# A transformer block on one core: each stage's first loads issued in the stage before it

## The chip, the cores and the metric

The kernel runs on one core of one Trainium2 chip. The metric is the device time in microseconds of one execution; the median of three runs counts. The engines are PE (TensorE, matrix products; PEld its weight loads), DVE (VectorE), ACT (ScalarE), POOL (GpSimd) and SP (SyncE, which here only issues DMAs, in the order of its program). They meet through semaphores.

## What is computed

One block on x of 1024 tokens by 1024 features, in float32: a half-weighted FFN, a mixer made of sparse attention (8 heads of 64) and an RWKV-7 recurrence (8 heads of 64), cross attention to 256 memory tokens, and a second FFN. Cut to what matters:

```python
x = x + 0.5 * rms_norm(swiglu(rms_norm(x, g), w_gate, w_up, w_down), g_post)      # FFN 1, D_FF 2816
proj = rms_norm(x, mix_pre_g) @ w_in                                              # 25 chunks of 128 columns
o_nsa  = nsa_mixer(q, k_c, v_c, k_s, v_s, k_w, v_w, gate_logits, ...)             # keys and queries rotated
o_rwkv = rwkv7_mixer(r, k, v, w_lo, a_lo, g_lo, ...)                              # (y + bonus) * g
x = x + rms_norm(concat([rms_norm(o_nsa, nsa_out_g), o_rwkv]) @ w_out, mix_post_g)
m = rms_norm(mem, mem_kv_g)
x = x + rms_norm(memory_cross_attention(rms_norm(x, mem_pre_g), m, wq, wk, wv, wo), mem_post_g)
x = x + 0.5 * rms_norm(swiglu(rms_norm(x, g), w_gate, w_up, w_down), g_post)      # FFN 2
```

## The kernel before

Every dense product is made of three passes of PE: each operand is split into a high part (ACT casts it) and a low part (DVE subtracts the high part from the original), and high x high, high x low and low x high are summed. So no product starts before its weights are loaded, cast by ACT and subtracted by DVE.

The work is in five stages, each a block of one program per engine, each with its own tiles in SBUF and its own semaphores: FFN 1 (`ffn_products`, L103), the front (`project_and_prepare`, L1756), attention with the recurrence (`attend_and_recur`, L1042), the memory stage (`memory_tail`, L2543) and FFN 2. Between two stages `Core.clear` (L66) sets the stage's semaphores back to zero on four engines, in a block of its own; a stage ends only when SP has waited for all of its stores. `block_kernel` (L2938) calls them.

FFN: SP loads a pair of 2 x 1 MB (256 columns of w_gate and of w_up, `load_pair`, L248) into `raw`, then loops over 11 pairs. FFN 2 begins with it. In FFN 1 the last loop (L319 to L326) goes over eight tiles of x: store tile t, load tile t + 3; DVE adds, normalises, and PE transposes for the next stage.

Front: 41 chunks of weights, 0.5 MB each, loaded by `load` (L1869) into two `raw` buffers in turn; a load waits until DVE has done the subtraction of the chunk two before. Chunks 0 to 24 are w_in, for all 1024 tokens (48 matmuls of 512 columns each). Chunks 25 to 32 are mem_wv and 33 to 40 mem_wk, for the 256 memory tokens (24 matmuls of 256 columns each). Rotated keys and queries, the recurrence's operands (`ops`, four of them), its values, gates and bonus are stored to DRAM for the stages behind. The transposed and split memory tokens lie in the first 256 columns of `hi` and `lo`. The memory keys are stored by one DMA when all chunks are done (L1961: waits for 41 evictions), the memory values (vm) by one of 1 MB after two transposes. After its first subtraction DVE waits for 14 small vectors (`first_steps`, L2286). The order on every engine is that of a plan (`front_plan`), which a list scheduler makes out of events with durations and dependences; SP's order too. `tail_plan` does the same for the memory stage, `joint_plan` for attention.

Attention: SP loads the recurrence's operands of two chunks of 64 tokens (eight DMAs of 128 KB), the first queries (four), keys (four of 0.5 MB) and compressed keys `kc` (two), values `vs` and `vw`, `vc`, V of two chunks (four DMAs), the second and third queries (eight). ACT issues seven small mask loads and four larger ones. PE's order begins with the products `gram_b` of chunks 0 and 1, `gram_k`, `gram_l`, three turns, then `x`, which needs V, and then the first scores, which need queries and keys. DVE waits for all seven masks before its first operation.

Memory stage: product 0 to 3 multiply the mixed tokens with w_out (8 slabs of 0.5 MB, two `raw` buffers), each of them with 8 slabs x 4 banks x 3 matmuls; 4 to 7 are the queries, 8 to 11 the output. Before product 0, DVE and ACT mix the tokens in four quarters (`mix_o`, `mix_y`, `mix_hi`, `mix_lo`), with gate and bonus loaded by quarter. All products use the same four PSUM banks, so product n waits for the evictions of n - 1 (L2678). `load_x` of tile 0 (L2640) brings two gain rows, km, vm and x, 3.5 MB in all.

## Time and profile before

| | us |
|---|---|
| three runs: lowest, median, highest | 2912.26, 2913.5, 2915.74 |
| the profiled execution | 2917.97 |
| its span, first to last instruction | 2916.2 |
| PE busy in it | 2721.9 |
| DVE, ACT busy | 1752.2, 969.1 |

Times of the profile are microseconds from the start of the span; a line of a timeline gives its start, its length, the engine, the source line, the operation, and in brackets how long the engine had been idle before it and what released it. SPq and ACTq are DMA issues. The granted clock of PE is its mean over a stretch, 1.00 being 2.4 GHz and 0.50 1.2 GHz. The mean over the execution is 0.959.

### The profile page before, as it was taken

How to read it: one execution, taken by the hardware profiler on the slowest of the kernel's cores; microseconds unless marked ns; L12 is line 12 of the kernel's file. 1: busy time of each engine (PE TensorE's matmuls, PEld its weight loads, DVE VectorE, ACT ScalarE, POOL GpSimd, SP SyncE). 2: the span in 40 equal slices, each digit the busy share in tenths (PEclk: the TensorE clock that was granted, in tenths of full speed). 3: DMA queues.
4: the chain of work that ended last, by engine and by line, in shares of the span. 5: the costliest groups of instructions: out<-in, count | busy, mean ns of one | idle time of the engine just before them, and what ended most of it. 6: DMA issues, size and time to landing. Idle time of an engine off the chain costs nothing. (4 is left out here: it accounts for less than half of the span.)

```text
span 2916.2 us, 47485 instructions
## 1 busy us (share of the span) xinstructions
PE 2721.9 (93%) x19432; PEld 2237.5 (77%) x19432; DVE 1752.2 (60%) x2865; ACT 969.1 (33%) x1732; POOL 87.2 (3%) x120
## 2 busy tenths in 40 slices
PE   6999999998899999589999998599996999999998
PEld 5888887886677778578888887477775788887887
DVE  5866666677243373267777775653453866666766
ACT  4322222214323343234444443342342322222112
POOL 0000000000000000111111110000000000000000
PEclk9999999999799999889999999799997999999999
DMA  3222223223422374621111100640112122223324
GB/s 135 80 86 87 83 79 108 87 101 145 94 73 79 109 242 128 169 71 42 35 35 35 35 9 5 213 150 2 44 71 91 61 80 83 86 83 109 112 89 151
DMA packets 230380, 260.65 MB, mean 89 GB/s; under 512 B 63300, under 2 KB 186435, under 8 KB 230212
## 3 DMA queue, kind: packets, MB, share of 16 engines
q1 hardware_dynamic: 228628, 256.65, 27.4%
q8 instruction: 124, 2.03, 0.3%
q10 hardware_dynamic: 1584, 1.60, 0.2%
q14 instruction: 44, 0.36, 0.0%
HBM read 188.91 MB, written 64.06 MB: 87 GB/s over the span
## 5 line engine op out<-in xcount | busy, mean ns | idle before, releaser
L709 PE MATMUL f_ps<-f_t1h,f_wh 128*128 128x512 f32 x480 | 187.1, 390 | 0.0
L710 PE MATMUL f_ps<-f_t1l,f_wh 128*128 128x512 f32 x480 | 186.7, 389 | 0.0
L2013 PE MATMUL fr_dense_ps<-one_hi,fr_wh 128*128 128x512 f32 x400 | 170.9, 427 | 11.3 <-DVE fr_wl L2298 11.3
L709 PE MATMUL f_ps<-two_hi,f_wh 128*128 128x512 f32 x384 | 150.6, 392 | 19.0 <-DVE f_wl L495 15.7
L2015 PE MATMUL fr_dense_ps<-one_hi,fr_wl 128*128 128x512 f32 x400 | 159.6, 399 | 0.0
L2014 PE MATMUL fr_dense_ps<-one_lo,fr_wh 128*128 128x512 f32 x400 | 159.6, 399 | 0.0
L709 PE MATMUL f_ps<-one_hi,f_wh 128*128 128x512 f32 x384 | 151.1, 394 | 8.7 <-DVE f_wl L495 4.6
L709 PE MATMUL f_ps<-f_t2h,f_t3h 128*128 128x512 f32 x384 | 151.1, 393 | 7.7 <-DVE ffn_y L601 3.7
L711 PE MATMUL f_ps<-one_hi,f_wl 128*128 128x512 f32 x384 | 150.7, 392 | 0.0
L710 PE MATMUL f_ps<-one_lo,f_wh 128*128 128x512 f32 x384 | 150.6, 392 | 0.0
L711 PE MATMUL f_ps<-f_t2h,f_t3l 128*128 128x512 f32 x384 | 150.4, 392 | 0.0
L710 PE MATMUL f_ps<-f_t2l,f_t3h 128*128 128x512 f32 x384 | 150.3, 392 | 0.0
L710 PE MATMUL f_ps<-two_lo,f_wh 128*128 128x512 f32 x384 | 150.1, 391 | 0.0
L711 PE MATMUL f_ps<-two_hi,f_wl 128*128 128x512 f32 x384 | 149.9, 390 | 0.0
L2687 PE MATMUL mt_d_ps<-mt_wh,two_hi 128*128 128x512 f32 x256 | 108.2, 423 | 33.9 <-DVE two_lo L2877 23.5
L603 DVE TENSOR_TENSOR y<-f_ps,y 128x512 f32<-128x512 f32 x144 | 99.2, 689 | 62.1 <-PE f_ps L711 62.1
L343 ACT CAST f_wh<-f_raw 128x1024 fp32r<-128x1024 f32 x60 | 63.0, 1053 | 219.5 <-PE f_ps L711 208.3
L543 DVE TENSOR_TENSOR y<-f_ps,y 128x1024 f32<-128x1024 f32 x60 | 72.5, 1222 | 100.6 <-PE f_ps L711 100.6
L543 DVE TENSOR_TENSOR ffn_y<-f_ps,ffn_y 128x1024 f32<-128x1024 f32 x60 | 72.5, 1222 | 100.4 <-PE f_ps L711 100.4
L603 DVE TENSOR_TENSOR ffn_y<-f_ps,ffn_y 128x512 f32<-128x512 f32 x144 | 98.7, 689 | 56.0 <-PE f_ps L711 56.0
L711 PE MATMUL f_ps<-f_t1h,f_wh 128*128 128x512 f32 x320 | 124.5, 389 | 0.0
L2298 DVE TENSOR_TENSOR fr_wl<-fr_raw,fr_wh 128x1024 fp32r<-128x1024 f32 x41 | 50.1, 1222 | 99.0 <-ACT fr_wh L2169 99.0
(391 smaller groups left out, 6820.8 us busy)
## 6 DMA issues: line engine op xcount, KB each, us to landing
f_raw<-in_ffn_w_gate SPq DMA_DIRECT2D x22, 1024.0 KB, 5.4
f_raw<-in_ffn_w_up SPq DMA_DIRECT2D x22, 1024.0 KB, 7.8
f_raw<-in_ffn_w_down SPq DMA_DIRECT2D x22, 1024.0 KB, 4.8
f_raw<-act SPq DMA_DIRECT2D x22, 1024.0 KB, 4.8
fr_raw<-in_w_in SPq DMA_DIRECT2D x25, 512.0 KB, 4.0
act<-ffn_y SPq DMA_DIRECT2D x44, 256.0 KB, 2.0
act<-y SPq DMA_DIRECT2D x44, 256.0 KB, 2.0
arena<-x SPq DMA_DIRECT2D x16, 512.0 KB, 4.0
```

Of the source, the lines that this page charges most:

```text
L343: nc.scalar.copy(w_hi[:, SLOT[s]], operand(s)).then_inc(split_hi, 1)
L543: nc.vector.tensor_tensor(out, a, b, op).then_inc(joined, 1)
L603: nc.vector.tensor_tensor(y[part(m)], down_bank(m), y[part(m)], ALU.add).then_inc(added[m % 4], 1)
L709: nc.tensor.matmul(out, wh, xh, start=start, stop=False)
L710: nc.tensor.matmul(out, wh, xl, start=False, stop=False)
L711: return nc.tensor.matmul(out, wl, xh, start=False, stop=stop)
L2013: nc.tensor.matmul(dense_ps[:, b, cols], w_hi[:, b, k, :], hi[:, k, cols], start=(k == 0), stop=False)
L2014: nc.tensor.matmul(dense_ps[:, b, cols], w_hi[:, b, k, :], lo[:, k, cols], start=False, stop=False)
L2015: mm = nc.tensor.matmul(dense_ps[:, b, cols], w_lo[:, b, k, :], hi[:, k, cols], start=False, stop=(k == KD - 1))
L2298: nc.vector.tensor_tensor(w_lo[:, c % 2], raw[:, c % 2], w_hi[:, c % 2].bitcast(F32), ALU.subtract).then_inc(lo_split, 1)
L2687: mm = nc.tensor.matmul(dense_ps[b][:], lhsT[:, k, at], rhs[:, k, to], start=(k == 0 and x_ == 0), stop=(k == KD - 1 and x_ == 2))
```

## The change

Each stage gets a function `lead` that its SP program calls near its end, and that issues the first loads of the next stage. They signal on semaphores made by `lasting`, which no `clear` resets, and write to tiles that outlive the stage. In particular:

- FFN 1, after the store of x tile 1: the first two weight chunks of the front, into `y[:, 0:2]`, which is now the front's `raw` (its `krv` lies in the rest of `y`).
- Front, behind the loads of chunks 33 to 39: operands of chunk 0, operands of chunk 1 (four DMAs each), keys high, keys low (two DMAs of 0.5 MB each), queries 0, 1, 2 (four DMAs each). SP waits once, behind load 33, for 25 products and for the stores of operands and rotated rows. Keys and queries go into `hi`, so the memory tokens now lie in columns 0 to 511 of `lo`.
- Memory keys are stored chunk by chunk (eight DMAs of 128 KB), each after its own eviction.
- Attention, after its last loads: gate and bonus of quarter 0, slabs 0 and 1 of w_out and the two gain vectors of the memory stage.
- Memory stage, after the first store of its second round: the first pair of FFN 2.
- Memory stage: four slab buffers (two of them the former operand tiles), the companions of `load_x` tile 0 planned behind slab 7, and product 1 in the banks `pair_ps`, `t_ps`, `o_ps`; product 2 then waits for the evictions of product 0, and the first transpose for those of product 1.

```diff
-    def pool_dma_sems(self, name, n):
+    def lasting(self, name, n=1):
         return [self.nc.alloc_semaphore(name=f"{name}{i}") for i in range(n)]
...
-            load_pair(0)
+            if not begun:
+                load_pair(0)
...
                 sp.dma_start(x_out[of_tile(t), :], x_of(t)).then_inc(x_stored[t % 4], 16)
+                if t == 1 and lead is not None:
+                    lead(sp)
...
-                sp.dma_start(raw[:, c % 2], weights[:, :, COLS[c]:COLS[c] + P]).then_inc(raw_in[c % 2], 16)
+                if c >= 2:
+                    sp.dma_start(raw[:, c % 2], weights[:, :, COLS[c]:COLS[c] + P]).then_inc(raw_in[c % 2], 16)
+                if c == CHUNKS - 8:
+                    sp.wait_ge(multiplied, PROJECTED)
+                    for n in range(3):
+                        sp.wait_ge(op_stored[n], 16 * PAIRS)
+                    for b in range(2):
+                        sp.wait_ge(r_stored[b], 32)
+                        sp.wait_ge(rot_stored[b], 96)
+                if c >= CHUNKS - 8:
+                    lead(sp, c - (CHUNKS - 8))
...
-                    sp.wait_ge(evacuated, CHUNKS)
-                    sp.dma_start(km.rearrange("(c p) t -> p c t", p=P), km_sb).then_inc(mem_stored, 16)
+                    p = e[1]
+                    sp.wait_ge(evacuated, at[("memk", p)] + 1)
+                    sp.dma_start(km[p * P:(p + 1) * P, :], km_sb[:, p, :]).then_inc(mem_stored, 16)
...
-        event(("load_w", m), "sp", 0.5, m >= 2 and ("w_lo", m - 2), m and ("load_w", m - 1), late=3.0)
+        event(("load_w", m), "sp", 0.5 if m >= 2 else 0.0, m >= 4 and ("w_lo", m - 4), m and ("load_w", m - 1), late=4.0 if m >= 2 else 0.0)
...
-                event(("dense", n, k, b), "pe", 0.68, before, *ready, k == 0 and n and ("evac", n - 1, b))
+                room = k == 0 and n and n != 1 and ("evac", 0 if n == 2 else n - 1, b)
+                event(("dense", n, k, b), "pe", 0.68, before, *ready, room)
...
-                  idx == 0 and ("mix_y", QUARTERS - 1), r and ("stored", 0, t), late=3.0)
+                  idx == 0 and ("mix_y", QUARTERS - 1), idx == 0 and ("load_w", KD - 1), r and ("stored", 0, t), late=3.0)
...
+        raw = [raw01[:, 0, :], raw01[:, 1, :], ops[:, 0, :], ops[:, 1, :]]
...
+        def bank(n, b):
+            return (pair_ps[:, 0, :], pair_ps[:, 1, :], t_ps[:], o_ps[:])[b] if n == 1 else dense_ps[b][:]
...
+                    if n == TT:
+                        sp.wait_ge(scored, 32)
+                        sp.wait_ge(lo_split, 3 * KD)
+                        lead(sp)
...
+            def first_chunks(sp, y):
+                w_in = f["w_in"].rearrange("(k p) n -> p k n", p=P)
+                for c in range(2):
+                    sp.dma_start(y[:, c, :].rearrange("p (k n) -> p k n", n=P), w_in[:, :, COLS[c]:COLS[c] + P]).then_inc(chunk_in[c], 16)
+            def first_keys(sp, n):
+                if n < 2:
+                    AR, B, K = (x[n] for x in chunk_ops(ops))
+                    for which, dst in enumerate((AR[:, :, 0, :], B, K, AR[:, :, 1, :])):
+                        load_op(sp, n, which, dst, ops_dram, ops_in)
+                elif n < 4:
+                    load_keys(sp, n - 2, (rot_hi, rot_lo)[n - 2], hi, keys_in)
+                elif n < 7:
+                    load_queries(sp, n - 4, hi, rot_hi, rot_lo, q_in)
+            def first_mix(sp):
+                kv0, raw01 = early_parts(early)
+                for n, src in enumerate((gate_y, bonus_y)):
+                    sp.dma_start(kv0[:, n, :].rearrange("p (q t) -> p q t", q=PAIRS),
+                                 src.rearrange("(q p) t -> p q t", p=P)[:, :, 0:QW]).then_inc(mix_in[0], 16)
+                for m in range(2):
+                    sp.dma_start(raw01[:, m, :], f["w_out"][m * P:(m + 1) * P, :]).then_inc(slab_in[m], 16)
...
+            def first_pair(sp):
+                for n, w in enumerate((f["ffn2_w_gate"], f["ffn2_w_up"])):
+                    sp.dma_start(early[:, n], w.rearrange("(k p) n -> p k n", p=P)[:, :, 0:2 * P]).then_inc(pair_in, 16)
```

## Rows read from the trace of the kernel before

**Rows 1.** The page: busy time by engine, and a DMA issue (count, KB, landing).

```profile
PE 2721.9 (93%) x19432; PEld 2237.5 (77%) x19432; DVE 1752.2 (60%) x2865; ACT 969.1 (33%) x1732; POOL 87.2 (3%) x120
...
act<-ffn_y SPq DMA_DIRECT2D x44, 256.0 KB, 2.0
```

**Rows 2.** Who PE waited for: us in total, times, longest.

```profile
PE f_ps L709 <- DVE f_wl L495: 20.3, 2, 15.7
PE ar_ps L1327 <- DMA ar_AR<-ops: 19.2, 2, 14.6
```

**Rows 3.** Timeline, FFN 1 to front, the first load, cast, product, and DVE's wait.

```profile
738.39 0.39 SPq L1873 DMA_DIRECT2D fr_raw<-in_w_in  x1
742.67 1.04 ACT L2169 CAST fr_wh<-fr_raw 128x1024 fp32r<-128x1024 f32 x1 [7.88 <-DMA fr_raw<-in_w_in]
745.03 0.79 PE L2013 MATMUL fr_dense_ps<-one_hi,fr_wh 128*128 128x512 f32 x1 [11.35 <-DVE fr_wl L2298]
750.16 0.17 DVE L2288 TENSOR_SCALAR fr_mu<-fr_mu 128x14 f32<-128x14 f32 x1 [5.18 <-DMA fr_vecs<-in_rwkv_gn_b]
```

**Rows 4.** Timeline, last two evictions of the front, store, attention's first issues.

```profile
1202.05 0.37 ACT L2179 COPY fr_c_w<-fr_dense_ps 128x256 f32<-128x256 f32 x1 [1.12 <-PE fr_dense_ps L2036]
1205.42 0.37 ACT L2179 COPY fr_c_w<-fr_dense_ps 128x256 f32<-128x256 f32 x1 [2.99 <-PE fr_dense_ps L2036]
1205.82 0.37 SPq L1962 DMA_DIRECT2D km<-fr_c_w  x1
1213.74 0.42 ACTq L1493 DMA_DIRECT2D ar_m_gram<-in_m_gram  x1
1216.72 0.45 ACTq L1493 DMA_DIRECT2D ar_mean_all<-in_mean_all  x1
```

**Rows 5.** Timeline of attention's ramp: DVE's first two evictions, product x.

```profile
1222.10 0.69 DVE L1554 TENSOR_TENSOR ar_GB<-ar_ps,ar_m_gram 128x512 f32<-128x512 f32 x1 [19.91 <-PE ar_ps L1327]
1228.60 0.69 DVE L1554 TENSOR_TENSOR ar_GB<-ar_ps,ar_m_gram 128x512 f32<-128x512 f32 x1 [5.81 <-PE ar_ps L1327]
1244.20 1.97 PE L1327 MATMUL ar_ps<-ar_V,ar_GK 64*64 64x64 f32 x32 [9.61 <-DMA ar_V<-rv_tok]
```

**Rows 6.** DMA issues (KB, landing), 1160 to 1206; then windows (busy, clock, share, GB/s).

```profile
fr_raw<-in_mem_wk SPq DMA_DIRECT2D x8, 512.0 KB, 4.0
...
vm<-fr_krv SPq DMA_DIRECT2D x1, 1024.0 KB, 5.3
km<-fr_c_w SPq DMA_DIRECT2D x1, 1024.0 KB, 4.7
...
1180.00:1190.00 10.00, 5.38 (x38) 4.97 (x37) 2.45 (x2) 2.24 (x5) 0.00 (x0) 0.93 0.80 215
```

**Rows 7.** Timeline, attention to memory stage, and around the gap in product 0.

```profile
1821.92 1.06 ACT L2782 ACTIVATE arena<-arena 128x1024 f32<-128x1024 f32 x1
1826.82 3.26 DVE L2860 SCALAR_TENSOR_TENSOR y<-y,mt_gain,arena 128x256 f32<-128x256 f32 x8 [7.86 <-DMA mt_g_pre<-in_mem_pre_g]
1841.08 0.76 PE L2687 MATMUL mt_d_ps<-mt_wh,two_hi 128*128 128x512 f32 x1 [23.51 <-DVE two_lo L2877]
...
1856.17 0.69 SPq L2639 DMA_DIRECT2D mt_raw<-in_w_out  x1
1868.72 1.23 DVE L2887 TENSOR_TENSOR mt_wl<-mt_raw,mt_wh 128x1024 fp32r<-128x1024 f32 x1 [9.22 <-ACT mt_wh L2803]
1870.00 0.79 PE L2687 MATMUL mt_d_ps<-mt_wh,two_hi 128*128 128x512 f32 x1 [9.02 <-DVE mt_wl L2887]
```

**Rows 8.** Timeline and windows, memory stage to FFN 2: first load, cast, PE's rate.

```profile
2221.12 0.38 SPq L250 DMA_DIRECT2D f_raw<-in_ffn_w_gate  x1
2229.47 3.88 ACT L334 CAST f_wh<-f_raw 128x1024 fp32r<-128x1024 f32 x4 [11.08 <-DMA f_raw<-in_ffn_w_up]
...
2233.00:2237.00 4.00, 4.00 (x10) 3.18 (x11) 2.17 (x2) 1.63 (x2) 0.00 (x0) 0.56 0.15 29
2237.00:2245.00 8.00, 8.00 (x37) 6.61 (x36) 0.00 (x0) 0.00 (x0) 0.00 (x0) 1.00 0.76 250
```

More of the change, by code:

```diff
@@ L121, in ffn_products @@
     with core.stage() as ctx:
-        raw = sbuf(nc, ctx, f"{tag}_raw", [P, 2, KD, 2 * P])
+        begun = raw is not None
+        if not begun:
+            raw, raw_in = sbuf(nc, ctx, f"{tag}_raw", [P, 2, KD, 2 * P]), core.sem(f"{tag}_raw_in")
         w_hi = sbuf(nc, ctx, f"{tag}_wh", [P, 4, 2, 4, P], F32R)
@@ L274, in _ @@
                     load_first(t)
-            load_pair(0)
+            if not begun:
+                load_pair(0)
             if before:
@@ L1039, in joint_plan, with queries_of, chunk_ops, load_op @@
     return in_order(engine, takes, needs, tiling=tiling)
+def queries_of(hi):
+    return hi[:, 4:7, :].rearrange("p r (w h t) -> p r w h t", w=2, h=4)
+def chunk_ops(ops):
+    parts = [ops[:, j, :].rearrange("p (x c) -> p x c", c=CH) for j in range(2)]
+    return ([x[:, 0:2 * PAIRS].rearrange("p (q w) c -> p q w c", w=2) for x in parts], [x[:, 2 * PAIRS:3 * PAIRS] for x in parts],
+            [x[:, 3 * PAIRS:4 * PAIRS] for x in parts])
+def load_op(sp, c, which, dst, ops_dram, ops_in):
+    src = ops_dram[which].rearrange("(q p) t -> p q t", p=P)[:, :, c * CH:(c + 1) * CH]
+    sp.dma_start(dst, src).then_inc(ops_in[c % 2], 16)
+def load_queries(sp, g, hi, rot_hi, rot_lo, q_in):
+    for w, rot in enumerate((rot_hi, rot_lo)):
+        src = rot[g % 2 * 4 * DH:(g % 2 + 1) * 4 * DH, g // 2 * P:(g // 2 + 1) * P].rearrange("(h d) t -> d h t", d=DH)
+        for half in range(2):
+            sp.dma_start(queries_of(hi)[half * CH:(half + 1) * CH, g % 3, w].bitcast(F32), src).then_inc(q_in[g % 3], 16)
+def load_keys(sp, w, rot, hi, keys_in):
+    for n, row in enumerate((4 * P, 5 * P)):
+        src = rot[row:row + 2 * DH, :].rearrange("(g d) t -> d g t", d=DH)
+        sp.dma_start(hi[w * CH:(w + 1) * CH, 2 * n:2 * n + 2, :].bitcast(F32), src).then_inc(keys_in, 16)
 def attend_and_recur(core, tag, rot_hi, rot_lo, kc_hi_dram, kc_lo_dram, v_tok, vc_dram, gates,
-                     ops_dram, rv_dram, end_decay, consts, a, hi, oT, o_ms, yT, y_var):
+                     ops_dram, rv_dram, end_decay, consts, a, hi, oT, o_ms, yT, y_var,
+                     ops, ops_in, keys_in, q_in, lead):
     nc = core.nc
@@ L1169, in _ @@
         def _(sp):
-            def load_q(g):
-                for w, rot in enumerate((rot_hi, rot_lo)):
-                    src = rot[g % 2 * 4 * DH:(g % 2 + 1) * 4 * DH, of_tile(g // 2)].rearrange("(h d) t -> d h t", d=DH)
-                    for half in range(2):
-                        sp.dma_start(q[rows(half), g % 3, w].bitcast(F32), src).then_inc(q_in[g % 3], 16)
-            def load_op(c, which, dst):
-                src = ops_dram[which].rearrange("(q p) t -> p q t", p=P)[:, :, chunk(c)]
-                sp.dma_start(dst, src).then_inc(ops_in[c % 2], 16)
             def load_v(c):
@@ L2540, in tail_plan, with early_parts, memory_tail @@
     return in_order(engine, takes, needs, lag)
-def memory_tail(core, tag, a, oT, o_ms, yT, y_var, arena, gate_dram, bonus_dram, x1, x2, x3, km, vm, hi, lo, y, consts):
+def early_parts(early):
+    return [early[:, n].rearrange("p (a k) f -> p a (k f)", a=2) for n in range(2)]
+def memory_tail(core, tag, a, oT, o_ms, yT, y_var, arena, gate_dram, bonus_dram, x1, x2, x3, km, vm, hi, lo, y, consts,
+                early, ops, vectors, mix_in, raw_in, gain_in, g_pre_in, lead):
     nc = core.nc
@@ L2572, in memory_tail @@
         top, bias, den, rden = (small[:, n, :] for n in range(4))
-        gate = kv[:, 0:2, :].rearrange("p r (q t) -> p r q t", q=PAIRS)
-        bonus = kv[:, 2:4, :].rearrange("p r (q t) -> p r q t", q=PAIRS)
-        kT = kv[:, 0:2, :].rearrange("p a (c t) -> p (a c) t", t=MT)
-        v = kv[:, 2:4, :]
+        kv0, raw01 = early_parts(early)
+        raw = [raw01[:, 0, :], raw01[:, 1, :], ops[:, 0, :], ops[:, 1, :]]
+        gate, bonus = ([kv[:, n, :].rearrange("p (q t) -> p q t", q=PAIRS) for kv in (kv0, kv1[:])] for n in range(2))
+        kT = kv0.rearrange("p a (c t) -> p (a c) t", t=MT)
+        v = kv1[:]
+        gain, g_pre = vectors[:, 0:PAIRS], vectors[:, PAIRS:PAIRS + KD]
         x = arena[:, 0:2, :]
@@ L2959, in block_kernel @@
     core = Core(nc)
-    def hidden_pair(ctx, name):
-        return [sbuf(nc, ctx, f"{name}_{part}", [P, KD, T], F32R) for part in ("hi", "lo")]
     with ExitStack() as ctx:
@@ L2974, in block_kernel @@
             end_decay = sbuf(nc, mixer, "end_decay", [P, PAIRS, NCH])
+            vectors = sbuf(nc, mixer, "vectors", [P, PAIRS + KD])
+            ops = sbuf(nc, mixer, "chunk_ops", [P, 2, D])
+            hi = sbuf(nc, mixer, "hi", [P, KD, T], F32R)
+            chunk_in, ops_in, q_in, mix_in = (core.lasting(*n) for n in (("chunk_in", 2), ("ops_in", 2), ("q_in", 3), ("mix_in", 2)))
+            slab_in, (keys_in, gain_in, g_pre_in, pair_in) = core.lasting("slab_in", 4), core.lasting("early_in", 4)
```

148 lines of the change are left out of this document (71 added, 77 removed).

## The prediction

> **What bounds the kernel now.** I read the page first, then who waited for whom on PE, then the timeline at the four places where one stage hands over to the next, and last the DMA view of two of these. The page shows PE busy for 2721.9 of 2916.2 us [rows 1]: inside the stages it is full, and nothing in the diff takes matmuls away. What can move is the idle PE time, at most 194 us. The waits of PE name few causes [rows 2], and the timeline puts the long ones at the hand-overs: 11.35 us between FFN 1 and the front stage (A) [rows 3], 14.59 + 4.63 + 9.61 us between the front stage and attention (B) [rows 4, 5], 23.51 us and then 9.02 us at the start of the memory stage (C) [rows 7], 15.7 us before FFN 2 (D) [rows 2]. A hand-over is: last evacuation, the wait for stores, the clearing of semaphores, the first loads, the first splits. The change takes the loads out of this sequence. So I price each place by the engine that starts first once the loads are there.
>
> **A, FFN 1 to front.** The first two weight chunks are loaded in FFN 1's tail. Now SP issues the first at 738.39 and ACT's cast begins at 742.67, released by that DMA [rows 3]. ACT leaves the hand-over when SP does, so the cast moves forward by 742.67 - 738.39 = 4.3 us, the DVE subtraction and PE with it. Next to be late is DVE: after its first subtraction it waits for the 14 small vectors, until 750.16 [rows 3], and only then splits chunk 1. Those are still queued on SP behind where the two loads stood, so they are issued 1 to 3 us earlier, chunk 1 is ready at 751 at the latest, and PE has 48 matmuls of chunk 0 to do, over 11 us from 740.8 (the rate of [rows 8]). Covered. In FFN 1 the two loads (1.0 us of SP's queue, 1 MB) stand between a store of x and the load of x tile 4, which is added three tiles later, some 15 us; covered too, bound 2 us. Gain 4.3, between 2 and 4.6.
>
> **B, front to attention.** Three pieces.
> First the end: km, 1 MB, is stored at once after the last evacuation, issued 1205.82 and landed 4.7 later [rows 4, 6], so at 1210.5; the next stage starts 3.2 later, 1213.74 [rows 4]. By chunks the last store is 128 KB. The nearest row, 256 KB stores, land in 2.0 [rows 1]. I take 2.1: start at 1211.1, 2.6 earlier. Only that last one stands before a wait. The Trainium skill (DMA: Bandwidth & Descriptors, Bandwidth) asks for DMAs batched to 1 MiB or more, since small ones are dominated by fixed costs, which speaks against eight small stores; for the one that is waited for the rows disagree, 2.0 against 4.7.
> Second the ramp. With operands, keys and three groups of queries in place, PE's first products start at once. But DVE waits for the seven mask loads, which stay in this stage: the last is issued 2.98 after the start (1216.72) [rows 4] and DVE's first product is at 8.36 after it, at the latest then [rows 5]. I take 7.0 (5 to 8.4): 1218.1. From there the chain to the product x is as now: 0.7 for one more eviction, and from DVE's second at 1228.60 to PE's x at 1244.20 without its 9.61 wait for V, 6.0 [rows 5]. x at 1224.8 in place of 1244.20: 19.4 us. V must be in by then: its four loads stand behind two kc, two value and one vc load, no longer behind 20 others; issued about 6 after the start at 0.6 each, landing some 4 to 7 later, just in time. Their lateness is in the range.
> Third the price. 24 extra DMAs, 4.5 MB (operands 1, keys 2, queries 1.5) go on SP's queue between the weight loads of the last eight memory chunks, each group behind load c and ahead of load c+1. There two evictions are 3.4 us apart [rows 4], and a 0.5 MB load takes 4.0 to land, two buffers deep [rows 6], so there is hardly any slack: landing + cast 1.04 + subtraction 1.23 [rows 3, 7] is 6.3 for the 6.7 of two chunks. The row that shows what a bulk transfer ahead of a weight load does is that of vm: one store of 1 MB, 5.3 us, and in the 10 us behind it PE is busy for 5.38 at 215 GB/s [rows 6]. So a group of 1 MB costs up to 4.6 us of PE, and there are two such (keys), and five of 0.5 MB. Counted as bytes from the first of these loads: weights 4.2 MB, vm 1, km chunks 0.9, groups 4.5, 10.6 MB, at 215 GB/s [rows 6] 49 us, at 250 [rows 8] 42 us, where eight chunks of 3.4 and vm's hole of 4.6 make 32 us now; but what is queued behind the last weight load doesn't delay it, and not every group finds the queue full. Followed step by step, each transfer behind the one before (0.5 MB 2.0 us; 1 MB 3.4, vm's landing less the 2.0 that a landing holds beyond its transfer), I get the last weights 6 us later. I take 7 us of delay, 2 to 15. The Trainium skill, same page, Queues, rings and completion order, says each DMA engine consumes descriptors in ring order: with it a weight load does wait behind the group; the vm row agrees. SP's new wait at chunk 33 (25 products done, operands and rotated rows stored) is over long before by the same plan; behind it stand that group and load 34. Net 19.4 - 7 = 12.4 us, between 4 and 19.
>
> **C, attention to memory stage.** Gate, bonus, the gains and two slabs of w_out are already in. DVE starts now at 1826.82, released by the gain load; ACT's square root, the other input, begins 1821.92 and takes 1.06 [rows 7]. So DVE can start at 1823.1: 3.7 us. Then the 9.02 us stall: slab 6 is issued at 1856.17 behind two row gains, km, vm and x, 3 MB, and its product starts at 1870.00 [rows 7]. After the change x and its companions come behind slab 7, and four buffers let slabs run four ahead, so that wait goes; what is late next is DVE, which stood idle for 9.22 us there and is full before it [rows 7]. DVE's end of the eight slabs thus moves by 3.7 + 9.2 = 12.9. After a stall PE also runs its first 4 us at half clock: granted 0.56, 10 matmuls, where 8 us at 1.00 hold 37 [rows 8], so a stall costs 4 - 10 x 8/37 = 1.8 us on top. Some of that comes back: I take 13.5. The other banks for product 1 let it start without the evictions of product 0; no wait of before stands there, so nothing, and the added wait, first transposes behind product 1's evictions, has some 40 us of matmuls to hide in. Ends: 9 (the planner puts transposes and slabs less well), 20 (it brings product 0 ahead of the second quarter's mixing, three DVE passes of 1.23 and half of one of 3.26 [rows 7]).
>
> **D, memory stage to FFN 2.** The pair of 1 MB each is issued at 2221.12, ACT's cast starts 2229.47, released by it [rows 8]. With the pair in place the cast starts with the stage: 8.3 us, 7 to 9. The loads go out near the first store of round two, where nothing but x tiles, due over 20 us later, is queued behind.
>
> **Sum.** 4.3 + 12.4 + 13.5 + 8.3 = 38.5 us. The profiled execution took 2917.97: 2879.5. Scaled to the median of 2913.5: 2875.0. Attention, the products and both FFNs are full of matmuls, so each gain passes to the end.
>
> **Rivals.** (1) The front stage gives back what attention's start gains: each of the seven groups costs what vm did by its size (2 x 4.6 + 5 x 2.0 = 19). For: the 215 GB/s row. Against: some queue time is idle now. B is then nil, 2887. (2) The groups run beside the weights, no delay: 2868. For: a 0.5 MB load every 3.4 us is 155 GB/s, below the 215 to 250 that the queue moves elsewhere [rows 6, 8], and the row of vm may show a store's cost, not a queue's. By the Trainium skill, same page, Specifications, a core's limit at the HBM is about 358 GB/s, by which the 10.6 MB would fit in 30 us; no row here shows that rate. (3) Slower: SP's own issue becomes the bound in the memory chunks. An issue takes 0.37 to 0.69 in the rows [rows 4, 7], and only a queue that is full would hold it longer. To eat the 19.4 + 26.1 us gained, 24 issues must take about 45 + 20 (seven chunks' slack beside their own issue, 7 x 3.0) = 65 us, 2.7 each; from there on it is slower, and at 3 each it is 2920. Against: seldom is more than one group behind. (4) The DVE bound at C, or a late V at B, holds the starts: of C only 3.7 and of B 4 stay, 2893.
>
> **How the numbers follow.** Forecast 0.50, rival 1 0.17, rival 2 0.19, rival 3 0.04, rival 4 0.07, and 0.03 for something that cancels all. Sum of lower bounds: 2 + 4 + 9 + 7 = 22, of upper 4.6 + 19 + 20 + 9 = 53: 2891.5 and 2860.5; a little more on either side for what moves in the planned orders gives 2858 to 2892. A measurement of this kernel tells 0.2% (5.8 us) from no change: faster 0.93, same 0.03, slower 0.04.
>
> **What would show it.** PE waits on ops, w_in's first chunk and f_raw at the starts gone; attention's first DVE product released by the masks, not PE. In the memory chunks more PE idle on fr_wl than the 4 us now, about 7 more. At C no 9 us gap, DVE without a hole until the eighth slab. Wrong if weight loads there land in 4 us as before (rival 2) or beyond 8 (rival 1), or if the wait for V stays.

## The result and the profile of the changed kernel

| | us |
|---|---|
| changed kernel, four runs: lowest, median, highest | 2878.17, 2884.62, 2886.44 |
| kernel before, timed beside it | 2912.26, 2914.45, 2915.74 |
| ratio, 95% interval | 0.989, 0.9875 to 0.9905 |
| profiled execution of the changed kernel, its span | 2878.17, 2876.4 |

The change gains 29.8 us on the medians. I had predicted 38.5 and 2875.0. Timed again in a later session the changed kernel took 2885.13 (2883.06 to 2887.05, ratio 0.9887, 0.9869 to 0.9904). The profiled execution is the fastest of its runs, so its trace flatters the change: 39.8 us between the two spans. I therefore cut both traces at the same events and compare stretch by stretch. The third column of numbers is the mean of the traces that hold the same code in that stretch: the changed kernel twice, and the experiments that leave the stretch alone, five of them for M, S and R. Among these seven traces M lies between 65.9 and 70.0, so a difference of M against a single trace is good to some 2 us.

| stretch, us | before | changed | mean of its like |
|---|---|---|---|
| start to the end of PE's work in FFN 1 | 733.7 | 731.1 | 733.2 |
| PE's wait at A | 11.35 | 7.07 | 7.1 |
| first product of the front to the first eviction of the memory chunks | 407.9 | 408.8 | 408.5 |
| M: from there to the last eviction (16 chunks) | 52.5 | 66.9 | 67.6 |
| S: from there to attention's first mask load | 8.3 | 6.4 | 6.2 |
| R: from there to the eviction of product x | 31.6 | 15.7 | 16.6 |
| from there to ACT's square root in the memory stage | 576.6 | 570.1 | 573.0 |
| Z: from there to the first product of FFN 2 | 411.0 | 384.4 | 384.4 |
| from there to the end | 683.2 | 685.9 | 683 or 686 |

So B, which is M + S + R, went from 92.5 to 89.0 (90.4 on the mean): the ramp gained nearly all it was to gain, and the front gave most of it back. Z holds C and D, and gained 26.6. FFN 1 keeps its length, so the two loads that stand in it now cost nothing that these traces can tell (single traces lie between 731.1 and 734.5; the kernel without them, below, has 732.8).

The waits of PE in the changed kernel (us in total, times, longest), in the order A, front, B, C, D:

```profile
PE fr_dense_ps L2045 <- DVE fr_wl L2330: 7.1, 1, 7.1
PE fr_dense_ps L2066 <- DVE fr_wl L2330: 16.2, 7, 8.8
PE ar_ps L1347 <- PEq L69: 6.4, 1, 6.4
PE ar_ps L1347 <- DVE ar_GB L1574: 4.2, 1, 4.2
PE mt_d_ps L2729 <- DVE two_lo L2922: 18.9, 1, 18.9
PE mt_d_ps L2729 <- DVE mt_wl L2933: 1.7, 1, 1.7
PE f_ps L715 <- DVE f_wl L501: 11.8, 2, 7.2
```

The wait on `ar_AR` of [rows 2] is gone, and the one before FFN 2 fell from 15.7 to 7.2. What grew is the second line, PE's waits for the subtraction of weights in the memory chunks. The three lines that answer to it and to the last waits at C, in the kernel before:

```profile
PE fr_dense_ps L2034 <- DVE fr_wl L2298: 5.0, 4, 4.2
PE mt_d_ps L2687 <- DVE mt_wl L2887: 10.4, 3, 9.0
PE mt_pair_ps L2702 <- DVE y L2908: 3.4, 4, 1.1
```

The timeline at A, which answers [rows 3]:

```profile
738.15 0.79 PE L2045 MATMUL fr_dense_ps<-hi,fr_wh 128*128 128x512 f32 x1 [7.07 <-DVE fr_wl L2330]
744.82 0.17 DVE L2320 TENSOR_SCALAR fr_mu<-fr_mu 128x14 f32<-128x14 f32 x1 [6.72 <-DMA fr_vecs<-in_rwkv_gn_b]
745.70 1.23 DVE L2330 TENSOR_TENSOR fr_wl<-one_y,fr_wh 128x1024 fp32r<-128x1024 f32 x1
```

DVE still waits for the small vectors, and is done with chunk 1 at 746.9, while PE has work from 738.15 on: covered, as priced.

The memory chunks and attention's ramp, which answer [rows 4, 5]. First ACT's cast of the chunk behind the keys, the last eviction, the first mask load, DVE's first evacuation and that of product x; then the issues on SP's queue (start, length of all, count):

```profile
1187.12 1.04 ACT L2201 CAST fr_wh<-one_y 128x1024 fp32r<-128x1024 f32 x1 [10.64 <-DMA one_y<-in_mem_wk]
1213.87 0.37 ACT L2211 COPY fr_c_w<-fr_dense_ps 128x256 f32<-128x256 f32 x1 [3.31 <-PE fr_dense_ps L2068]
1220.23 0.39 ACTq L1513 DMA_DIRECT2D ar_m_gram<-in_m_gram  x1
1229.07 1.29 DVE L1574 TENSOR_TENSOR ar_GB<-ar_ps,ar_m_gram 128x512 f32<-128x512 f32 x2 [18.43 <-DMA ar_mean_all<-in_mean_all]
1235.92 0.84 ACT L1492 COPY ar_AX<-ar_ps 128x256 f32<-128x256 f32 x2
```

```profile
1164.75 4.36 SPq L1063 DMA_DIRECT2D chunk_ops<-ops  x4
...
1174.24 5.16 SPq L1078 DMA_DIRECT2D hi<-rot_lo  x2
...
1180.56 6.21 SPq L1071 DMA_DIRECT2D hi<-rot_hi  x2
1186.82 4.60 SPq L1071 DMA_DIRECT2D hi<-rot_lo  x2
```

ACT stands idle for 10.64 us until the weights land. Two key loads occupy SP for 5.16 us and four query loads for 10.8, where an issue takes 0.4 to 0.6 when the queue has room. Landing times and windows of that stretch, which answer [rows 6] (4.0 us for the weights, 215 GB/s in the busiest window):

```profile
one_y<-in_mem_wk SPq DMA_DIRECT2D x8, 512.0 KB, 6.7
...
hi<-rot_lo SPq DMA_DIRECT2D x2, 512.0 KB, 13.3
...
1170.00:1180.00 10.00, 7.86 (x64) 7.42 (x63) 2.45 (x2) 3.75 (x5) 0.00 (x0) 1.00 1.01 253
1180.00:1190.00 10.00, 1.17 (x8) 0.97 (x7) 1.22 (x1) 1.32 (x2) 0.00 (x0) 0.63 1.11 229
1190.00:1200.00 10.00, 6.90 (x37) 6.70 (x36) 1.23 (x1) 1.46 (x3) 0.00 (x0) 0.67 1.07 219
```

The numbers behind the length are busy times, with the count of instructions, of PE, PEld, DVE, ACT and POOL; then PE's granted clock, the share of the DMA engines and GB/s. The share is the time that packets took, summed over the 16 engines; packets overlap, and in windows of 1 us it goes up to 1.31. At 1.01 and 1.11 packets are under way on the engines nearly all the time, and PE is busy for 1.17 us of ten. In the third window PE works again, at a granted clock of 0.67: 37 matmuls in 6.90 us, where the window from 1160 (shown at the end) has 76 in 9.23. By that rate some 2.4 us go to the clock. PE's waits grew by 11.2 us (16.2 against 5.0) of the 14.4 by which M grew. The start of the memory stage and that of FFN 2, which answer [rows 7, 8]:

```profile
1806.05 1.06 ACT L2827 ACTIVATE arena<-arena 128x1024 f32<-128x1024 f32 x1
1820.77 0.77 PE L2729 MATMUL mt_d_ps<-mt_wh,hi 128*128 128x512 f32 x1 [18.95 <-DVE two_lo L2922]
1840.73 0.50 PE L2729 MATMUL mt_d_ps<-mt_wh,hi 128*128 128x512 f32 x1 [1.73 <-DVE mt_wl L2933]
...
2187.00 3.88 ACT L340 CAST f_wh<-early 128x1024 fp32r<-128x1024 f32 x4 [2.62 <-PEq L69]
2190.49 0.80 PE L715 MATMUL f_ps<-hi,f_wh 128*128 128x512 f32 x1 [7.22 <-DVE f_wl L501]
```

From the square root to PE's first product it takes 14.72 in place of 19.16 us, and in product 0 one wait of 1.73 stands where 9.02 and two smaller ones stood.

### The profile page after: what moved, and what is told of

It reads as the page before. It is cut to its first block and busy times, and to the rows that moved or that the text cites. A ratio compares the mean times of both kernels' runs of the same rounds, so it can differ in the third digit from the quotient of the medians.

```text
span 2876.4 us, 47494 instructions
## 1 busy us (share of the span) xinstructions
PE 2716.7 (94%) x19432; PEld 2233.6 (78%) x19432; DVE 1751.7 (61%) x2865; ACT 969.3 (34%) x1732; POOL 87.4 (3%) x120
## 5 line engine op out<-in xcount | busy, mean ns | idle before, releaser
L715 PE MATMUL f_ps<-hi,f_wh 128*128 128x512 f32 x768 | 301.8, 393 | 19.2 <-DVE f_wl L501 11.8
L717 PE MATMUL f_ps<-hi,f_wl 128*128 128x512 f32 x768 | 300.5, 391 | 0.0
L715 PEld LDWEIGHTS f_ps<-hi,f_wh 128*128 128x128 f32 x768 | 145.4, 189 | 52.1 <-issue 10.7
L2045 PE MATMUL fr_dense_ps<-hi,fr_wh 128*128 128x512 f32 x400 | 171.3, 428 | 7.1 <-DVE fr_wl L2330 7.1
L717 PEld LDWEIGHTS f_ps<-hi,f_wl 128*128 128x128 f32 x768 | 145.2, 189 | 30.6
L2047 PE MATMUL fr_dense_ps<-hi,fr_wl 128*128 128x512 f32 x400 | 160.1, 400 | 0.0
L549 DVE TENSOR_TENSOR one_y<-f_ps,one_y 128x1024 f32<-128x1024 f32 x60 | 72.5, 1222 | 100.5 <-PE f_ps L717 100.5
L609 DVE TENSOR_TENSOR one_y<-f_ps,one_y 128x512 f32<-128x512 f32 x144 | 98.8, 690 | 55.9 <-PE f_ps L717 55.9
L2729 PE MATMUL mt_d_ps<-mt_wh,hi 128*128 128x512 f32 x224 | 94.6, 422 | 20.7 <-DVE two_lo L2922 18.9
L715 PEld LDWEIGHTS f_ps<-f_t1h,f_wh 128*128 128x128 f32 x480 | 90.1, 188 | 18.6
```

The lines of the kernel that those rows point to most:

```text
L549: nc.vector.tensor_tensor(out, a, b, op).then_inc(joined, 1)
L609: nc.vector.tensor_tensor(y[part(m)], down_bank(m), y[part(m)], ALU.add).then_inc(added[m % 4], 1)
L715: nc.tensor.matmul(out, wh, xh, start=start, stop=False)
L717: return nc.tensor.matmul(out, wl, xh, start=False, stop=stop)
L2045: nc.tensor.matmul(dense_ps[:, b, cols], w_hi[:, b, k, :], hi[:, k, cols], start=(k == 0), stop=False)
L2047: mm = nc.tensor.matmul(dense_ps[:, b, cols], w_lo[:, b, k, :], hi[:, k, cols], start=False, stop=(k == KD - 1))
```

## What the experiments tell apart

The question was where B's gain went, and whether C's came from what I had named. All kernels start from the changed one.

**The groups taken out of the front.** Keys, queries and operands load at attention's start again.

```diff
-                if c == CHUNKS - 8:
-                    sp.wait_ge(multiplied, PROJECTED)
...
-                if c >= CHUNKS - 8:
-                    lead(sp, c - (CHUNKS - 8))
...
+            for c in range(2):
+                for which, dst in enumerate((AR[c][:, :, 0, :], B[c][:], K[c][:], AR[c][:, :, 1, :])):
+                    load_op(sp, c, which, dst, ops_dram, ops_in)
+            load_queries(sp, 0, hi, rot_hi, rot_lo, q_in)
```

> The changed kernel without the groups in the front stage: operands, queries and keys are loaded at the start of attention, in the order of the kernel before; the rest of the change stays, memory keys by chunk too. Three lengths are read from its trace: F, from the issue of the load of chunk 33 to the last eviction of the front (38.8 us before, 53.0 after); S, from there to the first mask load of attention (8.3 before, 6.4 after); R, from there to the copy of product x (31.6 before, 15.7 after). If the groups alone lengthen F and shorten R: F 39, S 6.4, R 31.5, and the time is 15.9 - 14.2 = 1.7 us above that of the changed kernel, 2886. If attention's first 160 us, which took some 6 us less after than before, owe that to the groups too, it is 6 more, 2892. If the groups did not lengthen F (something else, the chunked store or SP's new wait, did): F stays near 53, and the time is 2900.

Measured: 2891.12 (2885.34 to 2894.3; ratio 0.9911, 0.9892 to 0.9929); the load of chunk 33 to the last eviction took 41.8, M 55.7, S 5.7, R 33.5. So the groups cost the front about 12 us (67.6 - 55.7), shorten the ramp by 17 (33.5 against 16.6), and are worth 4.6 us by the traces and 6.0 by the medians, of two sessions, whose intervals touch. Attention behind the ramp took 574.1 here against 573.0, so the rival that the groups also shorten it is not borne out. The 1.7 us that I expected came from the first trace of the changed kernel alone, which is short in this stretch, and took the whole delay to be that of the groups. Another 3.2 of M (55.7 against 52.5) are there without the groups. What is left of the change there are the memory keys stored by chunk, each store on SP's queue behind a wait for its eviction and ahead of the next weight load. In exchange S is 2.6 shorter, as predicted.

**The same issues with an eighth of the bytes.** The full loads follow at attention's start.

```diff
+                        src = ops_dram[which].rearrange("(q p) t -> p q t", p=P)[0:EI, :, n * CH:(n + 1) * CH]
+                        sp.dma_start(dst[0:EI], src).then_inc(junk_in, 16)
```

> As the kernel without groups, but the 24 DMAs of the seven groups are issued at their places in the front stage with one eighth of their partitions (0.56 MB in place of 4.5), and thrown away; the full loads follow at the start of attention. If the bytes are what lengthens the front: F (issue of load 33 to the last eviction) is 39 to 42 us, and an issue of a group DMA stays at 0.4 to 0.6 us. If the number of issues on SP is the limit (24 of them, and each weight load behind its group): F is 48 or more. If it is the wait that SP makes behind load 33: F is over 45 with load 34 late.

```profile
1164.05 1.75 SPq L3045 DMA_DIRECT2D chunk_ops<-ops  x4
...
1205.52 0.37 ACT L2219 COPY fr_c_w<-fr_dense_ps 128x256 f32<-128x256 f32 x1 [2.50 <-PE fr_dense_ps L2076]
```

2891.16 in one execution; M is 56.1 and the length from load 33 on 42.2, both as without groups (55.7, 41.8). It isn't the number of issues and not the new wait: it is what the issues transfer. Bytes and packets are both down to an eighth here, so this run doesn't tell the one from the other. Four issues take 1.75 us, 0.44 each, and the next four 2.76 in place of 4.36.

**The same bytes on the other queue.** ACT issues each group behind a cast, and no weight load stands behind a group.

```diff
                     nc.scalar.copy(w_hi[:, c % 2], raw[:, c % 2]).then_inc(hi_split, 1)
+                    if c >= CHUNKS - 8:
+                        lead(act, c - (CHUNKS - 8))
```

> The changed kernel with the same 24 DMAs issued by ACT, each group right after the cast of the chunk behind whose load it stood, so that no weight load is queued behind a group; the bytes and nearly the times are the same. If a weight load is late only because it stands behind a group on SP's queue: it lands in 4 to 6 us and F is 39 to 45 us. If the 16 DMA engines are full and share themselves over both queues: a load lands in 6 to 9 us, the DMA share is 0.9 to 1.0 from the first group to the last, and F is 48 to 56. ACT's own issues, 24 by about 0.5 us, may cost up to 4 of F in either case, more if ACT is held by a full queue.

```profile
one_y<-in_mem_wk SPq DMA_DIRECT2D x8, 512.0 KB, 6.2
...
1170.00:1180.00 10.00, 8.84 (x73) 8.63 (x74) 2.58 (x3) 5.04 (x7) 0.00 (x0) 1.00 1.07 225
1180.00:1190.00 10.00, 2.06 (x18) 1.85 (x17) 1.22 (x1) 1.81 (x3) 0.00 (x0) 0.77 0.95 301
```

2883.17 in one execution, M 65.7: the delay is still there, the weights land in 6.2, the share is about 1. ACT's own issues account for a little of it (its evictions waited 1.9 us on them in the memory chunks; I had allowed up to 4), not for the 10 us above the kernel without groups. So the order on one queue, from which I had argued with the row of vm, is not the main cause; what is left are the transfers beside each other on the 16 engines, which both queues share. Whether the engines themselves bind or the memory behind them, no run separates. The Trainium skill (DMA: Bandwidth & Descriptors, Issuing engines are not separate DMA queues) says that DMAs started by different engines run on the same 16 DMA engines and interleave; this trace agrees, with 65.7 against 67.6. By ring order alone, the rule that I had cited, M would have been about 56 here.

**All groups behind the last weight load,** the memory keys stored by ACT.

```diff
+                if c == CHUNKS - 1:
+                    for n in (0, 1, 4, 2, 3, 5, 6):
+                        lead(sp, n)
...
+                        if KINDS[c][0] == "memk":
+                            p = KINDS[c][1]
+                            act.wait_ge(evacuated, c + 1)
+                            act.dma_start(km[p * P:(p + 1) * P, :], km_sb[:, p, :]).then_inc(mem_stored, 16)
```

> The changed kernel with all seven groups behind the last weight load (chunk 40), where no weight waits behind them, in the order operands 0, operands 1, queries 0, keys high, keys low, queries 1, 2; the chunks of the memory keys are stored by ACT, each behind its eviction, so that the last store doesn't stand behind 4.5 MB. If the delay of the front came from the groups alone: F is 39 to 40 us. The last weight load is issued some 10 us before the last eviction, and S is 6 to 10, so 16 to 20 us at 240 GB/s move 3.9 to 4.8 MB: the groups are in, or nearly, when attention starts, and R is 15.7 to 20. Sum against the changed kernel: -14 + (0 to 4) + (0 to 4), 2871 to 2879 with -14 to -6. If the gain is given back because the last store or SP's issues of the groups hold the end of the stage: S is over 14, and the time is that of the changed kernel, 2882 to 2888.

```profile
1201.67 0.37 ACT L2208 COPY fr_c_w<-fr_dense_ps 128x256 f32<-128x256 f32 x1 [3.50 <-PE fr_dense_ps L2065]
...
1209.78 3.58 SPq L1071 DMA_DIRECT2D hi<-rot_lo  x2
...
1216.65 5.91 PE L1347 MATMUL ar_ps<-chunk_ops 64*64 64x128 f32 x64 [15.02 <-PEq L69]
```

2882.75 (2879.43 to 2884.73; ratio 0.9887, 0.9871 to 0.9904): no gain that these runs can tell. M is 53.8, within 1.3 of the kernel before, so the groups and the key stores on SP's queue hold all of the front's delay but 1.3 us. But S is 14.9: SP is busy with the 24 issues until 1213.4, and a stage ends only when SP has come to the end of its program. Of 13.8 us won in M, 8.7 went into S; the 4.7 that are left of M + S + R in the trace are 2.4 in the medians.

**The groups in small pieces, and earlier.** Operands behind chunks 26 and 27, keys in eight pieces of 256 KB behind chunks 29 to 37, four of the query loads behind 38 and 39, the rest behind the last weights; keys of the memory stored by ACT.

```diff
+            PIECE = {c: i for i, c in enumerate((29, 30, 31, 32, 33, 34, 36, 37))}
...
+                if c in (26, 27):
...
+                        load_op(sp, c - 26, which, dst, ops_dram, ops_in)
+                elif c in PIECE:
+                    w, m, half = PIECE[c] // 4, PIECE[c] // 2 % 2, PIECE[c] % 2
```

> The same 4.5 MB ahead of attention, but spread: operands behind the loads of chunks 26 and 27 (where the loads are 11 us apart), the keys in eight pieces of 256 KB behind the loads of chunks 29 to 34, 36 and 37, the first queries behind 38 and 39, the other queries behind the last weight load; the memory keys are stored by ACT. Lengths of the changed kernel, mean of five traces of it and of kernels alike in this stretch: memory chunks (first to last of their 16 evictions) 68 us, from there to attention's first mask load 6.3, from there to product x 16.5, 90.8 in all. If the delay came from more bytes in front of a weight load than its slack has room for (3.2 us a chunk, 0.5 MB of weights and 0.25 MB of keys are 234 GB/s, what the queue moves at its best): 53 to 56, 5 to 7, 16 to 17, so 15 us less, 2867 to 2873. If any bytes beside the weights delay them in proportion: 58 to 64, and 2874 to 2880. If SP is held at the end by the queries behind the last load: 6.3 becomes 9 or more.

```profile
one_y<-in_mem_wk SPq DMA_DIRECT2D x8, 512.0 KB, 5.7
...
1170.00:1180.00 10.00, 9.36 (x76) 8.72 (x75) 3.55 (x3) 5.15 (x7) 0.00 (x0) 1.00 0.64 188
...
1205.80 0.37 ACT L2210 COPY fr_c_w<-fr_dense_ps 128x256 f32<-128x256 f32 x1 [3.21 <-PE fr_dense_ps L2067]
...
1220.08 1.29 DVE L1574 TENSOR_TENSOR ar_GB<-ar_ps,ar_m_gram 128x512 f32<-128x512 f32 x2 [17.52 <-DMA ar_mean_all<-in_mean_all]
```

2871.97 (2869.34 to 2874.01; ratio 0.9842, 0.9828 to 0.9857), 13.2 us below the changed kernel timed beside it. M is 57.4, S 5.2, R 16.0, 78.5 in all against 90.4. M sits at the edge between the two expectations: 3.6 us of delay stay against the kernel that has all groups behind the last load. This kernel changes several things at once: the size of the keys' pieces, the place of the operands (before the first memory chunk is evicted) and of two groups of queries (behind the last weights), and who stores the memory keys. What each of them gives is not told apart.

**The masks too.** Two masks are loaded by ACT in the front, two others have their own semaphore, and V comes first in attention.

```diff
+            def first_mask(act, c):
+                if 29 <= c < 31:
+                    act.dma_start(masks[c - 29][:], f[MASKS[c - 29][0]]).then_inc(first_masks, 16)
...
-            dve.wait_ge(masks_in, 16 * 7)
+            dve.wait_ge(first_masks, 16 * 2)
```

> As the kernel with small pieces, and what was late next in attention's ramp moved as well: the two masks that the first products need are loaded by ACT in the front stage, the two next ones are the first that ACT loads in attention, on a semaphore of their own, and V of two chunks is the first that SP loads there. In the changed kernel DVE's first evacuation waited for the last of seven masks, 8.8 us after the start of attention, PE for it 4.2 us. If the masks alone held the ramp: the start to product x shrinks from 16.5 to 10 to 12, so 4 to 6 us less than with small pieces alone, 2862 to 2868. If V is late instead (four loads of 64 KB issued in 2.5 us, 5 or more to land): 14 to 16, and 1 to 2 us less.

```profile
1205.01 0.37 ACT L2219 COPY fr_c_w<-fr_dense_ps 128x256 f32<-128x256 f32 x1 [3.61 <-PE fr_dense_ps L2075]
...
1212.33 0.69 DVE L1580 TENSOR_TENSOR ar_GB<-ar_ps,k_m_gram 128x512 f32<-128x512 f32 x1 [10.54 <-PE ar_ps L1349]
...
1220.69 0.84 ACT L1496 COPY ar_AX<-ar_ps 128x256 f32<-128x256 f32 x2
```

DVE's first evacuation is now released by PE. S + R is 15.7 in place of 21.2, so the trace shows the 5.5 us that were expected of the masks (V moved too, but PE had waited for V in neither kernel). The times show less: 2870.42 (2863.4 to 2873.22; ratio 0.9837, 0.9822 to 0.9852), 1.6 below the small pieces alone, with intervals that overlap, and outside the 2862 to 2868 that I expected. That the masks held the ramp is shown; that moving them is worth 5 us of the whole is not. It is the fastest kernel of the study by its median.

**What removed the gap at C.** Three kernels undo the number of slab buffers, the place of the companions of x tile 0, and both; a fourth undoes the banks.

```diff
-        event(("load_w", m), "sp", 0.5 if m >= 2 else 0.0, m >= 4 and ("w_lo", m - 4), m and ("load_w", m - 1), late=4.0 if m >= 2 else 0.0)
+        event(("load_w", m), "sp", 0.5 if m >= 2 else 0.0, m >= 2 and ("w_lo", m - 2), m and ("load_w", m - 1), late=4.0 if m >= 2 else 0.0)
...
-                  idx == 0 and ("mix_y", QUARTERS - 1), idx == 0 and ("load_w", KD - 1), r and ("stored", 0, t), late=3.0)
+                  idx == 0 and ("mix_y", QUARTERS - 1), r and ("stored", 0, t), late=3.0)
```

> The changed kernel, but a slab of the memory stage is loaded only when the subtraction of the slab two before is done (before: the same; changed: four before); the companions of x tile 0 stay behind slab 7. Two lengths are read: Q, from ACT's square root at the start of the stage to the end of DVE's eighth subtraction (51.4 us before, 37.35 after), and Z, from that root to the first product of FFN 2 (411.0 before, 384.4 after). If the order alone removed the gap (no 3 MB in front of slab 6): Q is 37 to 40 and Z 384 to 387. If four buffers removed it: Q is over 44 and Z over 390.

> The changed kernel with four slab buffers, but the companions of x tile 0 (two gain rows, km, vm, x: 3.5 MB) may be loaded before slab 7, as in the kernel before. If four buffers alone are enough to cover the gap (the slabs run ahead of these loads): Q (root to the end of the eighth subtraction) is 37 to 40, Z (root to FFN 2's first product) 384 to 387. If the order is what counts: a wait of some 9 us comes back, Q 44 to 47, Z 391 to 395.

> The changed kernel with both undone: slabs two ahead, and the companions of x tile 0 before slab 7 if the plan puts them there. The early start and the other banks stay. If the two together removed the gap: a wait of about 9 us for slab 6 or 7 comes back, Q is 46 to 48 and Z 393 to 396. If the early start or the banks removed it: Q stays at 37 to 40.

PE's waits for the subtraction of slabs, with two buffers, then with both undone:

```profile
PE mt_d_ps L2729 <- DVE mt_wl L2933: 4.2, 1, 4.2
```

```profile
PE mt_d_ps L2729 <- DVE mt_wl L2933: 9.9, 2, 6.0
```

Two buffers (2890.91, one execution as are the next three): Q 41.6, Z 389.2, between the two expectations. Companions allowed early, four buffers (2883.89): Q 37.35, Z 384.48, the same as the changed kernel to 0.1; SP's order came out the same, since with four buffers the planner puts the slabs first anyway. Both undone (2900.28): Q 48.8, Z 397.9, some 2 us beyond what I expected. So four buffers alone take away the whole gap, the order alone takes 8.7 of 13.4 us, and the two don't add.

> The changed kernel with product 1 in the same four banks as all others, waiting for the evictions of product 0, and the first transpose without its wait. I priced the other banks at nothing. If that is right: Q 37 to 38 and Z 384 to 386. Rival: without them the planner brings evictions and mixing of quarters into product 0's way, or PE waits for product 0's evictions, which start only when DVE is done with the mixing: Z is 2 to 8 us longer.

```diff
-            return (pair_ps[:, 0, :], pair_ps[:, 1, :], t_ps[:], o_ps[:])[b] if n == 1 else dense_ps[b][:]
+            return dense_ps[b][:]
```

```profile
PE mt_d_ps L2729 <- DVE mt_wl L2930: 2.9, 3, 2.0
PE mt_pair_ps L2744 <- DVE y L2951: 3.2, 4, 1.0
```

2890.70; Q 39.3, Z 388.0: the other banks are worth 3.6 us. PE's waits account for 2.7 of them: 1.2 on slabs and 1.5 on `y` ahead of the transposes (1.7 in the changed kernel).

**A and D undone together.**

> The changed kernel with the loads ahead undone at A (first two chunks of the front) and D (first pair of FFN 2), each back in its own stage. As I priced them: PE's wait at A goes from 7.1 back to 11.35, that at D from 7.2 back to 15.7, so 12.8 us more, 2897 (2892 to 2902 with the scatter of one execution). Rival: a part of the two gains is given back later, as the loads stand between x tiles there: then less than 10 us come back.

```profile
PE f_ps L714 <- DVE f_wl L500: 20.3, 2, 15.7
...
PE fr_dense_ps L2044 <- DVE fr_wl L2329: 11.6, 1, 11.6
```

2898.49 in one execution, 13.4 above the changed kernel's median; the waits are back at 11.6 and 15.7. Nothing of the two is given back elsewhere.

**The changed kernel again.**

> The changed kernel once more, timed beside the others: 2884.6 is its median so far, with 2878 the lowest of four. I expect 2883 to 2887. Its trace is a second look at the lengths that differ between executions: attention from product x to the end (570 us in its first trace, 572 to 575 in all kernels that are alike there) and FFN 2 (683.2 in the kernel before, 686 in the changed one). If the clock is behind both: a 570 or 683 turns up in either kernel without a change of work.

2885.13, as expected. Windows of FFN 2, nearly the same stretch of the changed kernel in its first trace and of the kernel with small pieces (they begin 354 and 350 us behind FFN 2's first product):

```profile
2544.50:2644.50 100.00, 96.67 (x414) 79.52 (x413) 60.01 (x60) 29.24 (x33) 0.00 (x0) 0.97 0.29 100
```

```profile
2534.00:2634.00 100.00, 96.72 (x427) 79.73 (x426) 60.97 (x63) 28.55 (x33) 0.00 (x0) 1.00 0.29 100
```

FFN 2 took 683.0 to 683.3 us in four traces (before and three of the kernels derived from the changed one) and 685.9 to 687.1 in the others, with the same code. In the pair shown the long one has a granted clock of 0.97 where the short one has 1.00, which is 3 us of these 100. As both lengths turn up with the change, I take it as a scatter of 3 us and not its doing, though the kernel before has but one trace. Attention took 572 to 575 in this trace and its like, so the 570 of the first trace was scatter; whether the 576.6 of the kernel before is its true length can't be told from its one trace.

## Why the prediction was right, and where it was not

- **A and D, right.** 4.3 and 8.5 us against 4.3 and 8.3, and their covers held. They are the simplest case: the engine that starts first waited for a load, and the load was moved to where nothing was queued.
- **B, start and ramp, right but for the masks.** The store by chunk brought the start 2.1 us forward (2.6 predicted), the ramp shrank by 15.0 to 15.9 (16.8). Late next were the masks, as said, but later than priced: DVE's first product came 8.84 after the start, and 9.0 to 10.0 in the six traces like it, where I had 7.0 and at most 8.4. The upper end was where PE had released DVE in the kernel before, which only says that the masks were in by then in that trace. V was in time.
- **B, the price in the front, wrong by a factor of two.** I took 7 us, and it was 14.4, 15 on the mean, the end of my bound. B's net was 3.5 and 2.0 on the mean, where I had 12.4 and at least 4. At B, rival 1 with its 19 us was nearer than the forecast, and so it was in the whole: 2887 against the measured 2884.6, where the forecast said 2875.0. Two steps failed. I stacked the transfers one behind another at 2.0 us per 0.5 MB and 3.4 per MB, the rate of loads that run alone, (by the landings of [rows 6], 4.0 and 5.3 us, the second half MB adds 1.3 us and a landing holds 2.7 beyond, so the 2.0 was not read from rows; and 5.3 less 2.0 is 3.3), although my own other count, 10.6 MB at 215 to 250 GB/s against 32 us, gave 10 to 17 us; that was the better reading. I set it aside because bytes behind the last weight load delay nothing, but almost none were there. And I priced the stores of the memory keys only at the end of the stage. On SP's queue each of them waits for an eviction ahead of a weight load, which is most likely the 3.2 us that stay without groups: with the stores on ACT's queue and the groups last, 1.3 stay. Of the 14.4 us PE's waits are 11.2, where I forecast some 7 more than "the 4 us now" (the view has 5.0); the clock behind the long gap, which I priced at C and not here, is some 2.4 more. The median landing of the weights, 6.7 us, is between my two signs of being wrong, 4 and 8.
- **The mechanism at B, half wrong.** I saw the weights late because they stand behind a group in a queue. On a queue of their own they were just as late. What the runs leave is the sum of transfers on the 16 engines. By the windows of ten us (length by share), from 1160 on, packets took 22.5 of 46 us before and 50 of 60 after. But that is not 27 us of work that the groups brought: packets took longer beside one another. From 1160 to 1206, before and after (packets, MB, share):

```profile
q1 hardware_dynamic: 10785, 6.35, 48.6%
```

```profile
q1 hardware_dynamic: 17153, 10.51, 103.5%
```

That is 33 ns a packet before and 44 after (share times 46 us times 16, by the count), at 0.59 and 0.61 KB each; at 33 ns the 6368 packets more would have taken 13 us, in place of 25 (estimates from these two lines). Rival 3 (SP's issue) saw an effect that is real, issues of 2.6 us where 0.5 is normal, but only in the groups behind which some MB were outstanding; the run with an eighth of the bytes has them at 0.3 to 1.1. The trace of the kernel before already had it in attention's ramp, single issues of 5.49 (`vw`) and 6.36 us (`vc`), which I did not read.
- **C, undersized, at one term.** I had 13.5, it was 18.1 (26.6 less D's 8.5). The start gave 4.4 (3.7 predicted). Less that and D's 8.5, the 411.0 of the kernel before are 398.1; with four buffers and the new order but the old banks Z is 388.0, so these two gave 10.1, where I had 9.8 (9.2 from DVE's hole and 0.6 of the clock). The banks gave the other 3.6, and here the step that failed is "no wait of before stands there, so nothing": 0.7 + 0.3 + 3.6 is the whole error of 4.6. How the banks do it is in part argued: PE had waited 0.7 us for evictions before, and the waits that come back with the old banks are 1.2 on slabs and 1.5 on `y`, so they seem to free DVE and the planner to order evictions, mixing and slabs otherwise. They are worth this much only once the gap is gone: with the gap back and the other banks kept, Z is 397.9, 0.3 below the 398.1. In PE's waits the gain at C is 4.4 + 8.7 (slabs) + 1.7 (transposes) + 0.7 (evictions), less 0.3 that is new. Of the other 2.9 the clock behind the gap makes up to 2.3: from 1870 to 1878 it was granted 0.71 before, while from 1830 on it is 1.00 in the changed kernel's windows of product 0. The window of the gap in the kernel before (the clock is the third number from the end):

```profile
1862.00:1872.00 10.00, 2.00 (x5) 1.62 (x6) 3.28 (x3) 3.89 (x4) 0.00 (x0) 0.62 0.76 295
```

- **The sum, in part luck.** 4.3 + 2.0 + 18.1 + 8.5 = 32.9 us, and 3 us of scatter in FFN 2 and a few in attention to either side: 29.8 measured. The two errors, +4.6 at C and -10.4 at B, are of opposite sign; without the first the gain would have been 25 us and the time 2889, still within the wide range of 2858 to 2892, but near its end.

## What to carry to other kernels

In this kernel a load moved ahead of a stage was free where the DMA engines had idle time (A, D) and not where they had little. That is read from their share in windows, not from the queue in which it stands and not from the gaps of the engine that computes. Pieces no bigger than what one iteration leaves over, starting as early as the data exists, did better: with the same 4.5 MB the memory chunks grew by 15 us in seven groups and by 5 in small pieces, partly put elsewhere, the stores of the keys included. What stands last on the issuing engine also counts, since here a stage didn't end before SP was through with its issues; and a second set of buffers or banks can be worth something even where no wait on it is seen, because it lets other work be ordered better.

## What was not expected of the hardware

At a share of 1.0 the 16 engines moved very different amounts. Two windows of the changed kernel, first one in the front, with weights and operands in rows of 512 and 256 bytes, then one in the memory stage, with km, vm, x and slabs in rows of 1 to 4 KB:

```profile
1160.00:1170.00 10.00, 9.23 (x76) 8.82 (x75) 3.32 (x3) 4.23 (x6) 0.00 (x0) 1.00 0.97 214
...
1846.00:1856.00 10.00, 10.00 (x46) 8.29 (x45) 8.37 (x10) 5.20 (x11) 0.00 (x0) 1.00 1.02 399
```

The DMA view counts 1330 packets for 3.99 MB in the second, 3.0 KB each; from 1164 to 1204 there are 14800 for 9.34 MB, 631 bytes each. The length of rows is the plainest difference, but no run varies it alone, and it is not all: from 1184 to 1190 the view counts 913 packets for 1.13 MB, 1.2 KB each, and only 188 GB/s at a share of 1.09. Packets of the same 4 KB took 346 ns there on the mean and 164 ns in the window from 1846. What slows them in the front stays open. So a count of bytes at one rate, as I made it, misjudges such a stretch; the share shows at least that there is no room left. The Trainium skill (DMA: Bandwidth & Descriptors, Specifications) gives about 358 GB/s as a core's limit at the HBM, which I had quoted; this window, on one core alone, is above it, and nearer to the 425 GB/s that the same page's section Bandwidth has for a single core with large transfers.
